# Output projection's weights loaded inside the delta rule, state steps reordered, one inverse copy on VectorE, near blocks dealt in pairs

## What is computed

```python
# delta rule: state S per head, one token after the other, forward and backward
def step(s, inp):
    r_t, w_t, k_t, v_t, kk_t, ak_t = inp
    sa = jnp.einsum('bhvk,bhk->bhv', s, kk_t)
    s = s * w_t[:, :, None, :] - sa[..., None] * ak_t[:, :, None, :] + v_t[..., None] * k_t[:, :, None, :]
    return s, jnp.einsum('bhvk,bhk->bhv', s, r_t)
...
# behind it: readout (layer norm per head, bonus, gate), then
#   h = h + gate * (mixed @ w_out)           w_out is 1024 x 1024
#   router: softmax over 4 groups and 8 experts of each, two experts of one group
#   h = h + gate * sum over experts of comb * ((silu(x@w_gate) * (x@w_up)) @ w_down)
#   each expert has 3 matrices of 1024 x 512: 32 * 3 * 2 MB = 201 MB are read
```

## Time and profile before

| | us |
|---|---|
| median of 3 runs | 1783.94 (1781.68 to 1788.37) |
| the profiled execution, its own time | 1787.01 |
| its span, first to last instruction | 1785.2 |

### The profile page before, as it was taken

The page is one execution under the profiler, slowest core; times in us unless marked ns, Lnnn a source line. Parts: engine busy times, 40 slices in busy tenths (PEclk is TensorE's granted clock), DMA queues, the critical chain, the costliest instruction groups (busy, mean ns, idle before and its releaser), DMA issues.

```text
span 1785.2 us, 31410 instructions
## 1 busy us (share of the span) xinstructions
PE 1574.3 (88%) x13883; PEld 1259.2 (71%) x13883; DVE 839.8 (47%) x1127; ACT 652.5 (37%) x850; POOL 135.6 (8%) x105
## 2 busy tenths in 40 slices
PE   8999999999999999999998999988899765765576
PEld 7999998998799999899987987666654222212221
DVE  4444566665544455666656685885433101110111
ACT  4345545544344443455536223566512000000000
POOL 0600000000051000000001462000000000000000
PEclk9999999999999999999999999999999878788779
DMA  8553457755666525678552341000299999999998
GB/s 309 195 189 119 142 207 253 284 189 191 213 242 239 189 71 180 229 284 291 189 165 82 96 114 36 24 3 3 91 416 407 423 423 427 426 425 424 427 426 325
DMA packets 132323, 418.28 MB, mean 234 GB/s; under 512 B 14186, under 2 KB 35501, under 8 KB 113762
## 3 DMA queue, kind: packets, MB, share of 16 engines
q1 hardware_dynamic: 131762, 416.14, 61.5%
q10 hardware_dynamic: 432, 0.22, 0.0%
HBM read 414.45 MB, written 1.89 MB: 233 GB/s over the span
## 4 chain that ended last, share of the span: by engine, by line
PE 59%; DMA 19%; DVE 10%; ACT 6%; SPq 3%; issue 3%; DVEq 0%; ACTq 0%
PE ps_q L1423 17%; DMA R<-w_exp_down 17%; PE ps_p L1423 16%; SPq L1312 3%; PE ps_s L1538 3%; PE ps_t L1538 3%; ACT w_high L2147 2%; PE ps_p L1594 2%; PE ps_t L1594 2%; PE ps_s L1594 2%; DVE w_low L2639 1%; PE ps_q L1594 1%; PE ps_s L2086 1%; PE ps_t L2086 1%; DMA wring<-w_up 1%
## 5 line engine op out<-in xcount | busy, mean ns | idle before, releaser
L2639 DVE TENSOR_TENSOR w_low<-wring,w_high 128x2048 fp32r<-128x2048 f32 (+1 forms) x127 | 287.6, 2264 | 296.5 <-ACT w_high L2147 296.0
L2147 ACT ACTIVATE w_high<-wring 128x2048 fp32r<-128x2048 f32 (+1 forms) x127 | 236.3, 1860 | 325.2 <-PE ps_q L1423 147.4
L2069 PE MATMUL ps_q<-R 128*32 128x512 f32 x640 | 138.6, 712 | 107.3 <-DMA wring<-w_exp_up 64.8
L2069 PEld LDWEIGHTS ps_q<-R 128*32 128x32 f32 x640 | 34.4, 128 | 199.8 <-issue 128.6
L1423 PE MATMUL ps_q<-x_high,w_high 128*128 128x256 f32 x864 | 173.6, 282 | 1.3 <-DVEq L2690 1.3
L1423 PE MATMUL ps_q<-x_low,w_high 128*128 128x256 f32 x864 | 172.3, 281 | 0.0
L1423 PE MATMUL ps_q<-x_high,w_low 128*128 128x256 f32 x864 | 171.3, 279 | 0.0
L1423 PE MATMUL ps_p<-x_high,w_high 128*128 128x256 f32 x736 | 147.7, 282 | 2.2 <-DVEq L2690 1.9
L1423 PE MATMUL ps_p<-x_low,w_high 128*128 128x256 f32 x736 | 146.7, 281 | 0.0
L1423 PE MATMUL ps_p<-x_high,w_low 128*128 128x256 f32 x736 | 145.9, 279 | 0.0
L2069 PE MATMUL ps_q<-wring,R 128*32 128x512 f32 x384 | 138.4, 710 | 0.0
(11 more groups left out here) (802 smaller groups left out, 3018.3 us busy)
## 6 DMA issues: line engine op xcount, KB each, us to landing
wring<-w_in SPq DMA_DIRECT2D x29, 2048.0 KB, 8.2
R<-w_exp_up SPq DMA_DIRECT2D x24, 2048.0 KB, 37.2
R<-w_exp_down SPq DMA_DIRECT2D x23, 2048.0 KB, 44.4
wring<-w_up SPq DMA_DIRECT2D x22, 2048.0 KB, 8.0
R<-w_exp_gate SPq DMA_DIRECT2D x16, 2048.0 KB, 34.7
wring<-w_exp_gate SPq DMA_DIRECT2D x16, 2048.0 KB, 33.0
wring<-w_ada SPq DMA_DIRECT2D x12, 2048.0 KB, 10.1
wring<-w_down SPq DMA_DIRECT2D x10, 2048.0 KB, 7.8
```

What stands on the lines that cost most here:

```text
L2069: mm = pe.matmul(banks8[2 + which][q, :], xg[:, k, q], weight(u, k), start=k == 0, stop=k == KT - 1)
L2147: a.activation(high_of(l, job), half_block(l, job, wring), ACT.Copy).then_inc(w_high_ready, 1)
L2639: v.tensor_tensor(half_block(l, job, w_low), half_block(l, job, wring), high_of(l, job).bitcast(F32), ALU.subtract).then_inc(w_low_ready, 1)
```

## The change

It does six things. (1) w_out is loaded in pieces inside the delta rule: half 1 in five transfers once group 1's GT is made and its PH taken, into areas of the ring that groups 0 and 1 no longer use, `pB_a` and the up-projection's weights; half 0 in two transfers once NN of group 3 is made and a third once PH of group 2 is taken, into the last block of R. The two halves have their own semaphores (slots 11 and 10). (2) The expert slots are used in another order, and the counts of `moe_used` come from other points: 2 behind PS of group 3 instead of 3 behind GT, 3 behind the readout, 2 behind job bT, 1 behind projection job 1. (3) XV of groups 2 and 3 is copied out by DVE instead of ACT. (4) From step 28 on, parts 0 and 1 of a near pair lie behind `MXn` of group 2, 2 and 3 behind that of group 3, 4 behind `XMXn` of group 2, 5 behind that of group 3. (5) The state steps start behind "rc" and wait for PS rather than GT; `gate_out`, the readout's products and `bonus` are put behind state steps, two products of DVE for the bonus too; the readout is split in three: values, states (behind state steps 5 and 6 and behind "sa"), corrections (one direction at a time, each behind its own "sa"). (6) The output projection is made in the order 2, 3 (six k tiles each), bT, 0, 1.

```diff
-EXPERT_ORDER = (4, 2, 3, 5, 6, 7, 8, 0, 9, 1, 10, 11)
+W_OUT_LOADS, W_OUT_SLOT = (3, 5), (11, 10)
+EXPERT_ORDER = (1, 3, 5, 6, 7, 8, 9, 0, 2, 4, 10, 11)
-NEAR_AT = [int(n > 8 and n % 2 == 1) if n < 28 else 1 + int(n % 5 in (0, 3)) for n in range(len(GROUP_STEPS))]
+NEAR_AT = [int(n > 8 and n % 2 == 1) for n in range(28)] + [1, 1] + 6 * [2, 2, 1, 1] + [1, 1]
-        return [("T1", 8 * g + n, "act"), ("XV", 8 * g + n, "act")]
+        return [("T1", 8 * g + n, "act"), ("XV", 8 * g + n, "act" if g < 2 else "dve")]
+        half_in_ring = {0: (0, 5 * T2), 1: (0, 6 * T2), 4: (0, 7 * T2), 5: (2, 5 * T2), 6: (2, 6 * T2), 7: (2, 7 * T2)}
+        def w_out(half, k, n=1):
+            if half == 0:
+                return R[:, R_SIZE - BLOCK + 512 * k:R_SIZE - BLOCK + 512 * (k + n)]
+            if k in half_in_ring:
+                slot, o = half_in_ring[k]
+                return wring[:, slot, o:o + 512 * n]
+            return pB_a if k == 2 else R[:, ups_at:ups_at + 512]
...
-            wait_full2(sp, ("GT", 3))
-            for half in range(2):
-                name, c, width = BLOCKS2[half]
-                sp.dma_start(w2(half), ...).then_inc(loaded[half], 16)
+            def load_w_out(half, k, n):
+                sp.dma_start(w_out(half, k, n)..., w_out2[:, k:k + n, ...]).then_inc(loaded[W_OUT_SLOT[half]], 16)
+            wait_full2(sp, ("GT", 1))
+            wait_emptied2(sp, ("PH", 1))
+            for k, n in ((0, 2), (4, 1), (5, 3), (2, 1), (3, 1)):
+                load_w_out(1, k, n)
+            wait_full2(sp, ("NN", 3))
+            load_w_out(0, 0, 4)
+            load_w_out(0, 5, 3)
+            wait_emptied2(sp, ("PH", 2))
+            load_w_out(0, 4, 1)
...
+            def y_values(b, pr):
+                for c in lat:
+                    for hd in range(2):
+                        q = slice(64 * hd, 64 * hd + 64)
+                        for dr in range(2):
+                            pe.matmul(..., NN[q, 2 * dr + pr, 1, c, :], vtkh[q, pr, c, :], ...)
+            def y_states(b, i):
+                for pr in range(2):
+                    for dr in range(2):
+                        c, g = (i - 4, 7 - i)[dr], 2 * dr + pr
+                        for hd in range(2):
+                            q = slice(64 * hd, 64 * hd + 64)
+                            pe.matmul(..., rh[q, g, 64 * c:64 * c + 64], states[q, i, g, :], ...)
+            def y_corrections(b, dr):
+                for pr in range(2):
+                    g = 2 * dr + pr
+                    for c in lat:
+                        for hd in range(2):
+                            q = slice(64 * hd, 64 * hd + 64)
+                            mm = pe.matmul(..., NN[q, g, 0, c, :], nSA[q, g, c, :], ...)
+                return mm
...
-            gate_out()
-            wait_emptied2(pe, ("GT", 3))
             pe.wait_ge(state_ready, 1)
             for i in range(1, 7):
...
                 if i == 1:
-                    bonus()
+                    gate_out()
                 elif i == 2:
                     y_bank = open_bank("y", 0)
-                    y_out(y_bank, 0, True)
+                    y_values(y_bank, 0)
                 elif i == 3:
-                    y_out(y_bank, 1, True)
+                    bonus()
+                elif i == 4:
+                    y_values(y_bank, 1)
+                elif i == 5:
+                    y_states(y_bank, 4)
+                    y_states(y_bank, 5)
+                else:
+                    y_states(y_bank, 6)
                 wait_emptied2(pe, ("st", i))
+            wait_emptied2(pe, ("GT", 3))
...
-            wait_emptied2(pe, ("sa", 1))
+            y_states(y_bank, 7)
...
-            for pr in range(2):
-                mm = y_out(y_bank, pr, False)
+            for dr in range(2):
+                wait_emptied2(pe, ("sa", dr))
+                mm = y_corrections(y_bank, dr)
...
-            mix_out(0, (0, 1, 4, 5, 6, 7), False)
-            mix_out(1, (0, 1, 4, 5, 6, 7), False)
+            mix_out(2, (0, 1, 4, 5, 6, 7), False)
+            mix_out(3, (0, 1, 4, 5, 6, 7), False)
             pe.wait_ge(yb_ready, 1)
             b = fill("bT", 0)
...
-            mix_out(2, (0, 1), False)
-
+            mix_out(0, (0, 1, 4, 5, 6, 7), False)
             wait_emptied2(pe, ("bT", 0))
...
             mix_out(0, (2, 3), True)
+            mix_out(1, (0, 1, 4, 5, 6, 7), False)
             mix_out(1, (2, 3), True)
-            mix_out(2, (4, 5, 6, 7), False, begun=True)
             turn_h(0)
             mix_out(2, (2, 3), True)
-            mix_out(3, (0, 1, 4, 5, 6, 7), False)
...
+                elif stage[0] == "M" and g >= 2:
+                    job = ("XV", 8 * g + int(stage[-1]))
+                    b = full_bank(job).rearrange("p (n b t) -> p n b t", n=NCH // 2, b=2)
+                    v.tensor_copy(w.XT.rearrange("p (b n) t -> p n b t", b=2), b).then_inc(dve_emptied2, 1)
...
-            wait_emptied2(v, ("GT", 3))
-            v.memset(st[:, 61:62], 0.0).then_inc(moe_used, 3)
+            wait_emptied2(v, ("PS", 3))
+            v.memset(st[:, 61:62], 0.0).then_inc(moe_used, 2)
...
-            v.memset(st[:, 60:61], 0.0).then_inc(moe_used, 2)
+            v.memset(st[:, 60:61], 0.0).then_inc(moe_used, 3)
...
+            wait_full2(v, ("bT", 0))
+            v.memset(st[:, 62:63], 0.0).then_inc(moe_used, 2)
...
-                if j % 2 == 1:
-                    v.memset(st[:, 61:62], 0.0).then_inc(moe_used, 2 if j == 1 else 1)
+                if j == 1:
+                    v.memset(st[:, 61:62], 0.0).then_inc(moe_used, 1)
```

More of the change, by code:

```diff
@@ L209 @@
        (3456, 256), (3712, 256), (1280, 256), (1536, 256), (2048, 256), (1792, 256), (2304, 128)]
-BLOCKS2 = [("w_out_2", 512 * j, 512) for j in range(2)]
+W_OUT_LOADS, W_OUT_SLOT = (3, 5), (11, 10)
 N_BASE_DMA, N_EARLY_DMA, N_MOD_DMA = 13, 3, 2
-EXPERT_ORDER = (4, 2, 3, 5, 6, 7, 8, 0, 9, 1, 10, 11)
+EXPERT_ORDER = (1, 3, 5, 6, 7, 8, 9, 0, 2, 4, 10, 11)
 AREAS2 = (48, 6832, 17664, 23744, 27840)
@@ L362, in second_plan @@
     jobs += [("rc", 0, "dve")]
-    jobs += [("gg", 0, "act"), ("st", 1, "dve"), ("bon", 0, "act")]
-    jobs += [("st", i, "dve") for i in range(2, 7)]
+    jobs += [("st", 1, "dve"), ("gg", 0, "act"), ("st", 2, "dve"), ("st", 3, "dve"), ("bon", 0, "act")]
+    jobs += [("st", i, "dve") for i in range(4, 7)]
     jobs += [("sa", j, "dve") for j in range(2)]
@@ L769, in build @@
         wr = part(KT, 36)
+        ups_at = at[0]
         wup = part(B_W)
@@ L1022, in wait_wout @@
         def wait_wout(eng, half):
-            eng.wait_ge(loaded[half], 16 * (NB1 // SLOTS + 6))
+            eng.wait_ge(loaded[W_OUT_SLOT[half]], 16 * W_OUT_LOADS[half])
         def sem_of_in2(n):
@@ L1280, in _ @@
                              mod_at(2 + 3 * i, 0, [[0, P], [SLOTS_E * 512, 2], [1, 512]])).then_inc(gmul_in, 16)
[L1281 to L1284 removed]
+            w_out2 = d["w_out_2"][0].rearrange("(k p) n -> p k n", p=P)
+            def load_w_out(half, k, n):
+                sp.dma_start(w_out(half, k, n).rearrange("p (k n) -> p k n", k=n), w_out2[:, k:k + n, 512 * half:512 * half + 512])\
+                    .then_inc(loaded[W_OUT_SLOT[half]], 16)
+            wait_full2(sp, ("GT", 1))
[7 more added lines that the diff above has]
+            load_w_out(0, 4, 1)
             gates_d = [d[x].rearrange("a g e k n -> (a g e) k n") for x in ("w_exp_gate_2", "w_exp_up_2", "w_exp_down_2")]
@@ L1571, in mix_out @@
                 for k in ks:
-                    mm = pe.matmul(b[:, :], mixT[:, k, t * P:(t + 1) * P], w2(half)[:, k, :],
+                    mm = pe.matmul(b[:, :], mixT[:, k, t * P:(t + 1) * P], w_out(half, k),
                                    start=not last and not begun and k == ks[0], stop=last and k == ks[-1], skip_group_check=True)
@@ L1909, in bonus @@
                 mm.then_inc(full2, 1)
-            def y_out(b, pr, first):
+            def y_values(b, pr):
                 for c in lat:
@@ L2464, in group_step @@
                     take(("T1", 8 * g + int(stage[-1])), w.T1[:, :, :])
-                    take(("XV", 8 * g + int(stage[-1])), w.XT[:, :, :])
+                    if g < 2:
+                        take(("XV", 8 * g + int(stage[-1])), w.XT[:, :, :])
             for step, g in MIXER_STEPS:
@@ L3193, in _ @@
             v.wait_ge(rc_ready, 1)
-            for pr in range(2):
-                chain(v.scalar_tensor_tensor(ksum[:, pr, :], ksum[:, pr, :], col("rwkv_r_k_2", pr), pB_r[:, pr, :],
-                                             ALU.mult, ALU.mult))
-            v.memset(st[:, 63:64], 0.0).then_inc(bonus_in, 1)
             v.tensor_tensor(rbias[:, 0:36], full_bank(("rc", 0))[:, 0:36], rbias[:, 0:36], ALU.add).then_inc(dve_emptied2, 1)
-            wait_emptied2(v, ("GT", 3))
-            v.memset(st[:, 61:62], 0.0).then_inc(moe_used, 3)
+            wait_emptied2(v, ("PS", 3))
+            v.memset(st[:, 61:62], 0.0).then_inc(moe_used, 2)
             for dr in range(2):
```

(5 more changed lines are left out.)

25 lines of the change are left out of this document (9 added, 16 removed).

## The result

The changed kernel takes 1789.08 us (median of 14 runs, 1784.61 to 1791.14), the kernel before in the same comparison 1784.41 us (14 runs, 1781.68 to 1791.66): ratio 1.002, 95% interval 1.0011 to 1.003. So it is slower, by 2 to 5 us, where 1782.7 was forecast with a range up to 1789.0: just above its end, and on the other side. A later comparison of the two gave 1787.76 against 1783.61, ratio 1.0036 (1.0023 to 1.005). The profiled execution of after took 1788.69 us, its span is 1786.9.

The account below looks back on a forecast made before the run. Bound: the chain of engine work up to PE's first expert product, which releases block 12. Terms 0 - 1.3 + 0 + 2.1 - 0.5 - 2.75 + 1.2 = -1.2 us gave 1782.7 us, range 1773.5 to 1789.

Parts of the forecast that it names:

- What bounds it, and block 12: Expert stream: block 12 waits for PE's first use of an expert block; each us it moves, the end moves.
- the slots, w_out's two blocks and the projection's order: Expert stream and output projection: 0 us, two blocks (9.9 us) hide behind block 12's wait; same 32 products without a gap.
- The near loop, -1.3: Near pairs in the delta rule's levels: every pair takes 8.80 to 8.83 us, saving 1.3 us up to pair 6.
- the prediction's own last line: Signs of error: block 12 and end moving unequally, levels well below 8.8 us, or PE's clock below 1 in the levels.
- Transfers under a dense PE, +1.2: w_out transfers beside the rule's products: PE's program fetch stalls 0.47 us per block, 1.2 us together, bounds 0 and 4.9.
- XV on DVE, 0: Levels of groups 2 and 3: DVE's copy, taken as 0.676 us, is covered and costs 0 us.
- The end of the rule, +2.1: From pair 6's transposes to the rule's end: 1.5 us for a second Psi step, 0.6 for the W2 product.
- State steps and readout, -3.25: Behind the rule: state steps save 0.5 us, the readout 2.75; the 2.33 us stall stays in the sum.
- C: Rival, levels: PE's clock falls in each, five times 1.05 us, +4.1 in all, 1788.0 us; chance 0.14.
- B: Rival, levels: bound by ACT's queue, so 7.0 us a level instead of 8.8, -9 us, 1773.7; chance 0.12.
- A: Rival, state steps: the stall goes and PE's clock holds, 4.4 us more gained, 1778.3; chance 0.22.
- D: Rival, expert stream: its start sets the end, so the two w_out blocks count, -3 us, 1780; chance 0.04.

Follow-up runs that it names:

- e5: The changed kernel with two dummy products (0.26 us each) in PE's wait for XV of group 3: 1784.85 us, ratio 1.0003 to the kernel before.
- e7: The kernel before with only the changed state steps, readout, projection order and slots, w_out behind GT of group 3: 1782.69 us, ratio 0.9993.
- e13: The changed kernel with w_out's transfers held until XV of group 3 in level 1 is made: 1783.81 us, ratio 0.9997 to the kernel before.
- e4: The changed kernel with XV of groups 2 and 3 back on ACT: 1789.38 us, ratio 1.0029 to the kernel before.
- e3: The kernel before with XV of groups 2 and 3 copied by DVE alone: 1787.29 us, ratio 1.0015.
- e8: The kernel before with the changed state steps, readout, projection order and slots, and w_out inside the rule as changed: 1782.01 us, ratio 0.9994.

## Why the prediction was wrong, step by step

**What bounds it, and block 12**: right. In seventeen traces the span ends 429.0 to 430.2 us behind block 12's issue, over a spread of 13.7 us (1347.82 to 1361.51). What it said of the slots, w_out's two blocks and the projection's order holds with it: 49.97 us from the projection to block 12 before and after.

**The near loop, -1.3**: this is the step that failed, and by the prediction's own last line: PE's clock is below 1 in the levels. The price of one loop was right, 6.42 us from logits to transposes (1245.68 to 1252.10) and 8.81 a level, when the clock holds: pair 2 to 6 in e5 is 35.22 us, forecast 35.3. Two things were wrong. The 36.3 it was set against held one clock fall, which belongs to the execution and not to the dealing; with none, e7 has 34.74. So the dealing is worth +0.5 and not -1.0. And the levels were costed at full clock, though the text itself gave the gap of 1.4 with 0.4 behind it: the profiled after had four falls, +1.37 each, and its second execution two. Measured, pair 2 to 7 is 51.40 and 48.63 against 46.96 and 48.16, on average +2.5. Of the first piece, -0.3 up to pair 2, no more than 0.1 is seen where w_out is not in transfer (33.2 to 33.8 in the new dealing, 33.3 to 33.7 in the old).

**Transfers under a dense PE, +1.2**: right in mechanism, too small, the second term that failed. Its working spread 0.47 us over each of several program blocks; there was one stall of 2 to 3.6 us, with only half 1 in transfer beside the products (1211.4 to 1219), and after's ended as the first half of w_out had landed (252 GB/s in 1218 to 1220, 13 GB/s in the next 2 us). Five traces with the new dealing and the early w_out have stalls of 2.0 to 3.6 us; from pair 0 to 2 they take 36.8 on average against 33.4 for the four of that dealing without, +3.4, since the clock may fall behind the stall too. e13 gives 4 to 5 us in the medians. The upper bound of 4.9 held, and with the 3.4 in place of 1.2 the sum would have been +1.0. The stall's size comes from two parts of the change together: in the old dealing PE waits 0.94 us for ACT and turns pair 1 between those products, and the stall is 0.5 and 1.6.
The Trainium skill, "Runtime: NRT & Kernel Launch", section on instruction fetch mechanics, says that fetching is mostly hidden behind the pace of issue. At this place the measurement decides against it: the same products stall under 304 GB/s and not under 4, and PE goes on 1.3 us behind the late packet of its program.

**XV on DVE, 0**: right for the changed kernel (e4), not for the kernel before, where the same edit costs 1 to 5 us (e3). The copy takes 0.68 us, as taken.

**The end of the rule, +2.1**: over-priced by 0.8. From pair 6's transposes to rc 14.82 before, 16.15 after.

**State steps and readout, -3.25**: from rc to the projection -3.4 in the two first traces, on the average of two and two -2.5; but e7 and e8 gave only 1.3 to 2.0 in the medians, with wide intervals. The "issue" stall did not go: 1.81 us, and 1.12 more in "sa". Both vary from 0.4 to 3.1 between traces. They too end 1.3 to 1.6 us behind a packet of q8, but no run was made on them.

**The rivals.** C is what happened: its mechanism, place (the wait for XV of group 3) and side. Its price was 5 x 1.05, measured 4 and 2 x 1.37, and it had a chance of 0.14; its condition, that the wait must come near 1.96 us, was wrong. The clock falls behind 1.32, now and then behind 1.05 or 0.96, and holds behind 1.97 in e7. In the chances, B and a fifth of A make 0.16 and not 0.19. A did not come (1.81 remained), nor B (8.8 at full clock with ACT relieved), nor D (429 us stayed).

Put together from averages of two traces of each: pair 0 to 2 +2.3, 2 to 7 +2.5, the end of the rule +1.3, rc to the projection -2.5: +3.6 us. The medians say +4.7 and +4.2.

## What to carry to other kernels

Before a piece of the trace is used as the price of the old order, look whether a clock fall or a stall lies in it; it belongs to that execution, and a new order priced without one will look like a gain. A wait of PE that the timeline shows as free may not be: cost an order by its waits at both clocks, and where they can't be removed, a few dummy products that fit the wait (two, 0.6 us, for one of 1.3) hold the clock. Move bulk loads to where PE waits anyway, not under its densest run of small products; one wait of SP was worth 4 to 5 us in the new dealing, and nothing that shows in the old, where PE had a wait between the products.

## What the runs showed that was not expected

The granted clock fell to half behind waits of PE of 0.96, 1.05, 1.32 and 1.97 us in some executions and not in others of the same kernel, at a price of 1.4 to 1.5 us in a loop of 8.8. A stall under transfers at 304 GB/s, where PE waited for no other engine but for its own program, lasted 2 to 3.6 us, and moved to a level, where PE had to wait anyway, it cost nothing that can be seen. Pair 0 lies 4 us apart between executions, ahead of all that was changed.
